# Splitting expert weights into high and low parts with one instruction per tile in place of two

## The reference, cut to what matters

```python
scores = sigmoid(t @ w_router)                 # 64 experts, 8 chosen per token
...
for e0 in range(0, N_EXPERTS, EXPERT_BLOCK):
    hg = jnp.einsum('nd,edf->nef', t, w_gate[sl])     # D = 1024, F = 256
    hu = jnp.einsum('nd,edf->nef', t, w_up[sl])
    hw = jax.nn.silu(hg) * hu * combine[:, sl, None]
    routed = routed + jnp.einsum('nef,efd->nd', hw, w_down[sl])
shared = (silu(t @ ws_gate) * (t @ ws_up)) @ ws_down
x = x + g2 * (routed + shared)
```

## Time and profile before

| What | Value |
|---|---|
| Median of three runs | 1078.32 us (1072.11 to 1082.28) |
| Span of the profiled execution, first to last instruction | 1060.5 us |
| PE busy, share of the span | 953.4 us, 90% |
| DVE busy | 880.5 us, 83% |
| ACT busy | 611.8 us, 58% |
| POOL busy | 273.5 us, 26% |
| Moved by DMA | 286.27 MB, mean 270 GB/s |

### The profile page before, as it was taken

How to read it: one execution, slowest core, us unless ns; L and a number is a source line. 1 busy time by engine, 2 the same in 40 slices (tenths; PEclk the granted TensorE clock), 3 DMA queues, 4 the chain that set the end, 5 groups by cost and what they waited for, 6 DMA issues and landing times.

```text
span 1060.5 us, 14279 instructions
## 1 busy us (share of the span) xinstructions
PE 953.4 (90%) x4323; PEld 744.9 (70%) x4324; DVE 880.5 (83%) x1276; ACT 611.8 (58%) x961; POOL 273.5 (26%) x181
## 2 busy tenths in 40 slices
PE   1899999997999889999999999999998999899895
PEld 1654665876887568777778777787776777777773
DVE  4887775354548779999999999999998999999994
ACT  4215443554022157777777777776776777777672
POOL 1000205400000103242433423343333233333231
PEclk9899999588998999999999999999999999999998
DMA  9995222000044488999999999999999999999982
GB/s 351 396 381 206 80 79 109 1 1 1 40 178 184 132 308 286 368 368 340 342 357 344 370 352 342 361 349 359 322 345 353 314 345 365 360 359 352 358 290 48
DMA packets 93682, 286.27 MB, mean 270 GB/s; under 512 B 19497, under 2 KB 20009, under 8 KB 92753
## 3 DMA queue, kind: packets, MB, share of 16 engines
q1 hardware_dynamic: 71424, 248.04, 62.5%
q0 software_dynamic: 19056, 36.89, 13.9%
q10 hardware_dynamic: 3168, 0.94, 0.4%
HBM read 282.50 MB, written 37.88 MB: 302 GB/s over the span
## 4 chain that ended last, share of the span: by engine, by line
DMA 43%; PE 33%; DVE 11%; issue 8%; ACT 3%; POOL 1%; POOLq 0%; SPq 0%; DVEq 0%; ACTq 0%
DMA out<-oute,src_tab 31%; PE bank L613 9%; DMA xe<-h_rows,src_tab 6%; DMA w_gu<-in_w_exp_up 5%; PE bank L574 4%; PE bank L576 4%; PE bank L575 4%; DVE gu_low L1503 4%; PE bank L698 2%; PE bank L777 2%; PE bank L715 2%; DVE oute L1539 2%; POOL out L530 1%; DMA x_sb<-in_x 1%; PE bank L794 1%
## 5 line engine op out<-in xcount | busy, mean ns | idle before, releaser
L1503 DVE TENSOR_TENSOR gu_low<-w_gu,gu_high 128x1024 fp32r<-128x1024 f32 x256 | 301.6, 1221 | 9.7 <-ACT gu_high L1115 5.4
L1115 ACT CAST gu_high<-w_gu 128x1024 fp32r<-128x1024 f32 x256 | 256.7, 1055 | 76.4 <-PE bank L576 49.7
L530 POOL DMA_INDIRECT out<-oute,src_tab x64 | 133.2, 2081 | 426.7 <-DMA out<-oute,src_tab 291.1
L574 PE MATMUL bank<-gu_high,xeT_high 128*128 128x512 f32 x512 | 208.4, 407 | 4.5 <-DVE xeT_low L1503 4.2
L576 PE MATMUL bank<-gu_high,xeT_low 128*128 128x512 f32 x512 | 202.1, 395 | 0.0
L575 PE MATMUL bank<-gu_low,xeT_high 128*128 128x512 f32 x512 | 201.8, 394 | 0.0
L1503 DVE TENSOR_TENSOR d_low<-w_d,d_high 128x1024 fp32r<-128x1024 f32 x128 | 150.6, 1220 | 0.0
L1121 ACT CAST d_high<-w_d 128x1024 fp32r<-128x1024 f32 x128 | 128.3, 1056 | 12.9 <-PE bank L576 12.0
L574 PEld LDWEIGHTS bank<-gu_high,xeT_high 128*128 128x128 f32 x512 | 97.0, 189 | 26.3 <-issue 3.9
L574 PE MATMUL bank<-d_high,hwT_high 128*128 128x512 f32 x256 | 109.2, 427 | 6.7 <-DVE hwT_low L1503 6.5
L524 POOL DMA_INDIRECT xe<-h_rows,src_tab x64 | 100.6, 1571 | 53.2 <-DVE src_tab L1575 27.8
(11 more groups left out here) (283 smaller groups left out, 1277.1 us busy)
## 6 DMA issues: line engine op xcount, KB each, us to landing
w_gu<-in_w_exp_gate SPq DMA_DIRECT2D x128, 512.0 KB
w_gu<-in_w_exp_up SPq DMA_DIRECT2D x128, 512.0 KB
w_d<-in_w_exp_down SPq DMA_DIRECT2D x128, 512.0 KB
ada_w<-in_w_ada SPq DMA_DIRECT2D x8, 2048.0 KB
first_w<-in_w_ada SPq DMA_DIRECT2D x3, 2048.0 KB, 22.9
w_out_sb<-in_w_out SPq DMA_DIRECT2D x2, 2048.0 KB, 7.3
w_lat_sb<-in_w_in SPq DMA_DIRECT2D x1, 2688.0 KB, 23.2
x_sb<-in_x SPq DMA_DIRECT2D x1, 2048.0 KB, 13.7
```

The costliest lines, as they stand in the source:

```text
L530: pool.indirect_dma_start(out_rows, bass.IndirectOffsetOnAxis(ap=rows, axis=0), oute[i][:], None, bounds_check=last_row, oob_is_err=False, ...
L574: pe.matmul(dst, xh, wh, start=start, stop=False)
L1115: act.copy(gu_high[half][:, m], w_gu[half][i][:, m]).then_inc(gu_high_ok[half], 1)
L1503: return dve.tensor_tensor(low, whole, high.bitcast(F32), ALU.subtract)
```

## The change

Memory first: the eight PSUM banks were eight tensors and become views of four tensors of two banks each, at the same places, so that one instruction can read two neighbouring banks. Then each pair becomes one instruction: the casts and subtractions of each half of the gate and up weights (2 x 1024 to 2048 elements), of the down weights (the same), of the transposed rows (2 x 512 to 1024), and the `out_copy` (the same). The semaphore counts are halved to match: DVE's subtraction now waits for the whole cast. Buffers, loads, the order of work on each engine and the matmuls stay. The helpers serve the shared-expert phase's first casts and the extra blocks too.

```diff
-        bank = [ctx.enter_context(nc.psum_tensor(f"bank{i}", [P, BANK], F32)) for i in range(8)]
+        twin = [ctx.enter_context(nc.psum_tensor(f"bank{i}", [P, 2 * BANK], F32)) for i in range(4)]
+        bank = [twin[i // 2][:, i % 2 * BANK:(i % 2 + 1) * BANK] for i in range(8)]
...
-                wait(pe, xe_high_ok, times(n, 2))
-                wait(pe, xe_low_ok, times(n, 2))
+                wait(pe, xe_high_ok, n)
+                wait(pe, xe_low_ok, n)
...
             def gate_up_high(half, i, loads, n):
-                for m in range(2):
-                    act.copy(gu_high[half][:, m], w_gu[half][i][:, m]).then_inc(gu_high_ok[half], 1)
+                act.copy(gu_high[half][:], w_gu[half][i][:]).then_inc(gu_high_ok[half], 1)
             def down_high(i, loads, n):
-                for m in range(2):
-                    act.copy(d_high[:, m], w_d[i][:, m]).then_inc(d_high_ok, 1)
+                act.copy(d_high[:], w_d[i][:]).then_inc(d_high_ok, 1)
             def rows_high(i, n):
-                for m in range(2):
-                    act.copy(xeT_high[i][:, m * HC:(m + 1) * HC, :], bank[m][:].rearrange("p (c n) -> p c n", c=HC)).then_inc(xe_high_ok, 1)
+                act.copy(xeT_high[i][:], twin[0][:].rearrange("p (c n) -> p c n", c=C)).then_inc(xe_high_ok, 1)
...
             def gate_up_low(half, i, n):
-                for m in range(2):
-                    dve.wait_ge(gu_high_ok[half], times(n, 2) + (m + 1))
-                    last = lowered(gu_low[half][:, m], w_gu[half][i][:, m], gu_high[half][:, m])
-                last.then_inc(gu_low_ok[half], 1)
+                dve.wait_ge(gu_high_ok[half], n + 1)
+                lowered(gu_low[half][:], w_gu[half][i][:], gu_high[half][:]).then_inc(gu_low_ok[half], 1)
             def down_low(i, n):
-                for m in range(2):
-                    dve.wait_ge(d_high_ok, times(n, 2) + (m + 1))
-                    last = lowered(d_low[:, m], w_d[i][:, m], d_high[:, m])
-                last.then_inc(d_low_ok, 1)
+                dve.wait_ge(d_high_ok, n + 1)
+                lowered(d_low[:], w_d[i][:], d_high[:]).then_inc(d_low_ok, 1)
             def rows_low(i, n):
-                for m in range(2):
-                    dve.wait_ge(xe_high_ok, times(n, 2) + (m + 1))
-                    lowered(xeT_low[i][:, m * HC:(m + 1) * HC, :], bank[m][:].rearrange("p (c n) -> p c n", c=HC), xeT_high[i][:, m * HC:(m + 1) * HC, :]).then_inc(xe_low_ok, 1)
+                dve.wait_ge(xe_high_ok, n + 1)
+                lowered(xeT_low[i][:], twin[0][:].rearrange("p (c n) -> p c n", c=C), xeT_high[i][:]).then_inc(xe_low_ok, 1)
             def out_copy(i, n, stores):
-                for m in range(2):
-                    cols = slice(m * BANK, (m + 1) * BANK)
-                    last = dve.tensor_tensor(oute[i][:, cols], bank[4 + m][:], mod[:, GATE2, cols], ALU.mult)
-                last.then_inc(oute_ok, 1)
+                dve.tensor_tensor(oute[i][:], twin[2][:], mod[:, GATE2], ALU.mult).then_inc(oute_ok, 1)
```

More of the change, by code:

```diff
@@ L813, in gate_up @@
             def gate_up(i, n, before):
-                pe.wait_ge(xe_low_ok, times(n, 2) + 2)
+                pe.wait_ge(xe_low_ok, n + 1)
                 wait(pe, hw_ok, before)
```

## The result

The changed kernel took 1089.77 us (median of 4 runs, 1081.33 to 1104.85), the kernel before 1075.21 us (median of 4, 1063.49 to 1082.28). The ratio is **1.023, 95% interval 1.018 to 1.028**: slower, though whether by more than 2% the interval leaves open. Measured again beside two of the experiments (e10) it was 1.031 (1.021 to 1.041). The profiled execution has a span of 1085.5 us and a time of 1087.26 us; the span before was 1060.5.

What follows compares the result with a forecast made beforehand. The prediction took the chain of scatters, each waiting for the last to land, as the bound. Scatter hold +23, DVE -5, DMA -7, head and tail +1 made +12 us, 1078.3 to 1090 us; range 1069 to 1108, likeliest case 1083 to 1097.

Steps and rivals of the forecast that it cites:

- The bound: Expert loop: each scatter waits for the one before to land, pace 10.49 us per expert, little left for `oute`.
- The mechanism: POOL's scatter waits for DVE's two-SBUF subtraction to end; merged ones hold it 0.40 us more each, +23 us.
- the sample of five: Five scatters walked at the same phase against merged subtractions: sum 10.49 to 12.51 us, taken as fair.
- The DMA term: A slower pace asks less of full DMA engines, so landings come sooner: 0 to 13 us back, half taken, -7 us.
- DVE's saving: Five merged pairs save DVE 0.35 us per expert, counted only in 16 steps that `oute` ended: -5 us.
- The late expert: Rival, clearly slower: waiting for the whole cast makes `oute` 0.78 us later for late experts; +32 us, 1110, chance 0.15.
- Head and tail: First and last experts have no neighbours to hide a whole cast of 1.98 us instead of 1.055: about +1 us.
- The sum: All terms on the profiled span of 1060.5 us: +23 - 5 - 7 + 1 = +12 us.
- Faster: Rival: DVE sets each step and loses 0.35 us until PE stops it at 9.78; about 14 us, 1064, chance 0.10.
- no change: Rival: the scatters' phase against DVE shifts and the lock wait stays near 0.5 us; 1079 us, chance 0.28.
- The estimate by the fixed part for each merge: Rival: DVE regains its full fixed part per merge, 0.79 us per expert, 45 us, so 1033; chance 0.02.

Runs made afterwards that it cites:

- e10: The changed kernel run again with its file unchanged, beside two other experiments; 1.031 to the kernel before, 1099.32 us.
- e4: Kernel before with only the PSUM work merged (cast and subtraction of the transposed rows, `out_copy`), weights left in pairs; 1.001, 1074.31 us.
- e12: Changed kernel, but from the fifth expert the merged down subtraction reads an idle PSUM bank as second operand; 0.995 to the kernel before, 1060.12 us.
- e8: Changed kernel loading half the columns of each down matrix from expert 4 on, a sixth of weight bytes left out; 0.977 to before, 1054.96 us.
- e11: Changed kernel with SP's down load issued later, after the next load of half 0; 1.034 to the kernel before, 1102.08 us.
- e1: Kernel before with only the weight subtractions (gate, up, down) merged, waiting for the whole cast; 1.034, 1106.23 us.
- e5: Changed kernel with every weight subtraction in four pieces of 512 elements; 1.025 to the kernel before, 1103.10 us.
- e6: Changed kernel with gate and up subtractions in halves, only the down subtraction merged; 1.020 to the kernel before, 1093.08 us.
- e3: Kernel before, all in pairs, but the first subtraction of each pair waits for both casts; 1.003, 1069.89 us.
- e9: Changed kernel with the down subtraction in halves and the next expert's `hidden_low` moved between them; 0.995 to the kernel before, 1059.15 us.

## Why the prediction was right or wrong, point by point

**The bound** was read rightly: the chain of scatters. e4 makes DVE faster and changes nothing; e12 frees the scatter and wins it all back. The step was read from three landings (7.62 us); over 57 the landing takes 7.38, and the rest is waiting beyond the 0.81 us, in 18 of the 57 steps.

**The mechanism** was right: POOL held by longer two-SBUF subtractions. Its term was **+23 us** (0.40 per scatter) and measured **+18** (0.31). The rule did not overstate it, the sample of five did: the same walk over all 58 scatters of the kernel before, each at its own phase, gives 0.24 to 0.32, by how early in its instruction a scatter is taken to meet the lock (0 to 0.12 us after its start). The prediction also says that POOL gets in between the halves of a pair. Its own first row shows that it may not: the first half ended at 603.98 + 1.22 = 605.20, the scatter of 604.92 passed that end and ended 1.45 us after the second.

**The DMA term was wrong in sign**, and it is the step that failed: "A pace 3 to 4% slower asks less of full DMA engines", -7 us. The landing time rose by 0.20 us, +11, so this term alone is 18 us off. e8 shows that the load makes the landing time, so the reason was not empty, but something else outweighed it. When a merged `d_low` ends, it lets go both of POOL and of SP's next load, and the scatter's instruction ends 1.46 us later, behind that load. SP of the changed kernel, beside the scatter of 503.22, whose `d_low` ended at 504.56 and whose instruction ended at 506.02:

```profile
504.72 0.81 SPq L441 DMA_DIRECT2D w_d<-in_w_exp_down  x2
```

Count from the issue of the first of a load's two transfers to the end of the scatter's instruction. In the changed kernel this was over 1 us for all 57 scatters (landing 7.58). In the kernel before it was over 1 us for 43 of 57, which landed after 7.48 on the mean, and less for 14, which landed after 7.07; in e12, where POOL is free, it was less for 46, which landed after 6.85. With e8 and e11 aside, whose loads differ, the landing is also long where the scatter is held longest (7.50 to 7.63 in the changed kernel, e1, e5, e6 and e10) and shorter in the others (6.96 to 7.38). That is a correlation in the traces; e11 moved the load and the landing fell, but with a new wait, so it points that way without settling it. Why the landing rose stays open.

**DVE's saving** was put at -5 us by 16 steps that `oute` ended. The waiting beyond 0.81 us changed by -1 us in all: the 0.35 us per expert that DVE saved came back as its own waits for ACT (26.0 us idle before the merged gate and up subtractions against 5.7, 43.1 before `xeT_low` against 20.6). The late expert does show it; ACT and DVE of the changed kernel in order of time:

```profile
527.56 1.91 ACT L1115 CAST gu_high<-w_gu 128x2048 fp32r<-128x2048 f32 x1
```

```profile
529.57 2.29 DVE L1501 TENSOR_TENSOR gu_low<-w_gu,gu_high 128x2048 fp32r<-128x2048 f32 x1 [0.58 <-ACT gu_high L1115]
```

DVE starts at 527.56 + 1.91 + 0.10. That I counted at nothing, with the slack before the landing as cover, and e3 bears it out (1.003).

**Head and tail** were put at +1 us and measured -3.9 + 0.9 = -3. No run tells which part of that is the change.

**The sum** was +12 and measured +25 us of span, twice as much. The predicted 1090 us met the measured median of 1089.77 by luck, since a second error went the other way: I put 17.8 us around the span of the profiled execution, taking it for a median one. The changed kernel's profiled execution had 1.8 us around its span, so that of before probably took some 1062 us. Against it +25 gives 1087; the forecast's size should be judged by the ratio, 1.011 forecast, 1.023 to 1.031 measured.

**The rivals.** Faster and no change are out by the interval. The late expert is out as a cause (e3). The estimate by the fixed part for each merge (0.79 us per expert) does not hold: the merged `gu_low` is 0.07 shorter than its pair. What I had not seen is that only one of the three merged subtractions costs anything.

## What to carry to other kernels

Before merging or lengthening a DVE instruction with both operands in SBUF, look at what GpSimd issues beside it: if an indirect DMA on the critical chain starts while the DVE instruction runs, its own instruction is held until that one ends, and perhaps past it if another such instruction follows at once. Merge where few of the critical DMAs start (gate and up here), keep halves behind the instruction that releases it, or give one operand a place in PSUM. A faster instruction on a busy engine is worth what the chain of waits leaves for it, and a forecast must start from the time of the profiled execution itself, not from a median of others.

## What the runs showed of the hardware that was not expected

- GpSimd's indirect DMA waited for ends of DVE's two-SBUF instructions and then took 1.46 us (scatter), but it could miss an end when the next such instruction followed at once: with halves of 1.22 us 10 of 58 scatters passed one end, with quarters of 0.69 us 35 of 58 passed one to three, and the mean hold was no shorter (2.58 us) than with one instruction of 2.29 (2.43). No end that something other than a weight subtraction followed was passed, `hidden_low` between two halves included (31 of 31 got in, e9).
- A `tensor_tensor` of 2048 elements with one operand in PSUM took 2.276 us against 2.283 with both in SBUF: the same length, but no hold on GpSimd.
- Leaving out a sixth of the weight bytes (e8) brought the scatter's landing from 7.58 to 5.94 us after its instruction, with the DMA engines' share falling only from 0.98 to 0.95.
